# Layer one's input projection in another column order, with the compression products, turns and the compressed branch placed between its groups

## The reference

```python
proj = hn @ nsa_w_in                      # 2212 columns: q 768, kc vc ks vs kw vw 192 each, gates 36, memory q 256
q, ks, kw = rope(q), rope(ks), rope(kw)
kc = rope(compress(kc_raw)); vc = compress(vc_raw)     # 15 blocks of 32 tokens: gelu(x @ w1) @ w2
out = g0 * softmax(q kc) vc + g1 * softmax(q ks) vs + g2 * softmax(q kw) vw
mo  = softmax(q_mem mem_k) mem_v
h   = h + rmsnorm(concat(out, mo) @ w_out)
```

## Time and profile before

| what | value |
|---|---|
| median of 3 runs (lowest, highest) | 831.14 us (829.1, 834.99) |
| the profiled execution, its span | 830.26 us, 828.5 us |
| mean granted TensorE clock | 0.945 |
| busy: TensorE, VectorE, ScalarE, GpSimd | 754.0, 489.2, 407.2, 100.0 us |

### The profile page before, as it was taken

One profiled execution on the slowest core, in us unless ns is written; L12 is line 12 of the kernel. 1 busy time (PEld: TensorE's weight loads), 2 busy tenths in 40 slices (PEclk: granted clock), 3 DMA queues, 4 the chain that ended last, 5 costly groups with the idle time before them and its releaser, 6 DMA issues.

```text
span 828.5 us, 15559 instructions
## 1 busy us (share of the span) xinstructions
PE 754.0 (91%) x6725; PEld 653.9 (79%) x6725; DVE 489.2 (59%) x707; ACT 407.2 (49%) x644; POOL 100.0 (12%) x148
## 2 busy tenths in 40 slices
PE   4999856969999999999988976999989999999996
PEld 3888745657888888888868965999978888888885
DVE  5767653562686666643559696433456866666422
ACT  6744743553765554532767613332326845455411
POOL 4004042460000000000141003530000000000000
PEclk9999875789999999999989987899999999999999
DMA  9846600000765655555653323000006556555511
GB/s 301 297 131 207 222 29 1 1 1 9 233 210 184 203 173 183 203 191 164 186 183 102 107 98 103 3 4 5 4 2 229 169 187 203 171 185 203 183 71 52
DMA packets 78280, 111.74 MB, mean 135 GB/s; under 512 B 2125, under 2 KB 63715, under 8 KB 78211
## 3 DMA queue, kind: packets, MB, share of 16 engines
q1 hardware_dynamic: 77090, 107.67, 38.6%
q0 software_dynamic: 976, 3.04, 1.2%
q10 hardware_dynamic: 144, 0.04, 0.0%
HBM read 109.68 MB, written 1.05 MB: 134 GB/s over the span
## 4 chain that ended last, share of the span: by engine, by line
PE 68%; DVE 14%; ACT 6%; issue 2%; POOL 0%; DVEq 0%; ACTq 0%
PE ps L945 18%; PE ps L1084 10%; PE ps L947 9%; PE ps L666 8%; PE ps L667 7%; PE ps L668 7%; DVE w_lo L1688 3%; PE ps L821 2%; PE ps L795 1%; PE ps L772 1%; ACT scores L1327 1%; ACT w_hi L1251 1%; DVE row_max L1776 1%; DVE x_hi_lo L1913 1%; ACT x_hi_lo L1432 1%
## 5 line engine op out<-in xcount | busy, mean ns | idle before, releaser
L1688 DVE TENSOR_TENSOR w_lo<-w_raw,w_hi 128x2048 fp32r<-128x2048 f32 (+1 forms) x99 | 222.8, 2263 | 96.9 <-ACT w_hi L1251 96.7
L945 PE MATMUL ps<-x_hi_lo,w_hi 128*128 128x512 f32 x640 | 226.5, 399 | 0.0
L1251 ACT ACTIVATE w_hi<-w_raw 128x2048 fp32r<-128x2048 f32 (+1 forms) x99 | 185.4, 1890 | 50.7 <-PE ps L668 50.3
L947 PE MATMUL ps<-x_hi_lo,w_lo 128*128 128x256 f32 x640 | 179.7, 281 | 0.0
L945 PEld LDWEIGHTS ps<-x_hi_lo,w_hi 128*128 128x128 f32 x640 | 120.3, 188 | 29.9
L947 PEld LDWEIGHTS ps<-x_hi_lo,w_lo 128*128 128x128 f32 x640 | 120.9, 189 | 0.0
L666 PE MATMUL ps<-w_hi,x_hi_lo 128*128 128x512 f32 (+2 forms) x240 | 83.1, 346 | 3.5 <-DVE x_hi_lo L1913 3.0
L667 PE MATMUL ps<-w_lo,x_hi_lo 128*128 128x512 f32 (+2 forms) x240 | 81.6, 340 | 0.0
L668 PE MATMUL ps<-w_hi,x_hi_lo 128*128 128x512 f32 (+2 forms) x240 | 81.4, 339 | 0.0
L666 PE MATMUL ps<-w_hi,hidden_hi 128*128 128x512 f32 x176 | 68.6, 390 | 0.0
L667 PE MATMUL ps<-w_lo,hidden_hi 128*128 128x512 f32 x176 | 68.5, 389 | 0.0
(11 more groups left out here) (368 smaller groups left out, 1166.2 us busy)
## 6 DMA issues: line engine op xcount, KB each, us to landing
w_raw<-w_ffn_in SPq DMA_DIRECT2D x44, 1024.0 KB, 5.1
w_raw<-w_ffn_out SPq DMA_DIRECT2D x22, 1024.0 KB, 4.9
w_raw<-rwkv_w_in SPq DMA_DIRECT2D x11, 1024.0 KB, 5.4
w_raw<-nsa_w_in SPq DMA_DIRECT2D x8, 1024.0 KB, 12.1
w_raw<-w_out SPq DMA_DIRECT2D x8, 1024.0 KB, 5.0
w_raw<-w_mem_kv SPq DMA_DIRECT2D x2, 1024.0 KB, 8.4
w_raw<-nsa_cmp_k_w SPq DMA_DIRECT2D x2, 1024.0 KB, 5.4
w_raw<-nsa_cmp_v_w SPq DMA_DIRECT2D x2, 1024.0 KB, 5.4
```

Of the source, the lines that this page charges most:

```text
L945: pe.matmul(psum[:, bank + j, :], kt_of(w_hi, i, k)[:, c], xx[:, k, :, :].rearrange("p c n -> p (c n)"), start=k == 0, stop=False)
L947: ins = pe.matmul(psum[:, bank + j, 0:SEQ], kt_of(w_lo, i, k)[:, c], xh[:, k, :], start=False, stop=k == KD - 1)
L1251: act.activation(w_hi[:, i % SPL, 0:size(i)], raw[:, i % RAW, 0:size(i)], ACT.Copy).then_inc(hi_done, 1)
L1688: dve.tensor_tensor(w_lo[:, i % RAW, 0:size(i)], raw[:, i % RAW, 0:size(i)], w_hi[:, i % SPL, 0:size(i)], ALU.subtract).then_inc(lo_done, 1)
```

## The change

- The groups of the projection are `NSA_COLS` in the order 1, 2, 0, 4, 3: columns 512 to 1024, 1024 to 1536, 0 to 512, 1920 to 2212 (gates and memory queries, 292), and last 1536 to 1920 (window keys and values, 384). The compression's weights come before the last group, and so do its products, in banks 6 and 7.
- Turns stand at `between` points of the groups, by half and tile: memory keys in group 2, compression inputs in group 3, selected keys in group 4, queries between the two compression products, memory queries, `hidden_turns`, `block_mlp` and `block_key_turn` in group 5. A turn may have one column (`count`).
- The window keys are rotated after group 5 and turned in step 2 of the attention, through banks 4 and 5.
- The block scores move from step 4 to step 1, `block_probs` from 5 to 3, the block turns to steps 4 and 5, one tile each, both in bank 5.
- Memory outputs go to bank 6 + t.
- One weight piece and not three of the output projection is split before the attention; eight halves and not four are split within, from step 7 (VectorE) and not 12.
- The rotation order on VectorE, the copies of `vc_tok` on GpSimd, and the points of `turn_out` and `split_to` follow.

```diff
+NSA_COLS = [(0, 512), (512, 1024), (1024, O_KW), (O_KW, O_G), (O_G, NSA_IN)]
+NSA_ORDER = [1, 2, 0, 4, None, 3]
-        LAG_T, LAG_V, HALF_STEPS = 3, 4, 12
+        LAG_T, LAG_V, HALF_STEPS = 3, 4, 7
-                c = SEQ * (f - FT) + P * t
-                return 6, slice(c, c + P)
+                return 6 + t, slice(P * (f - FT), P * (f - FT) + P)
+        TURNS = [("mk", 0, 2), ("dup", 0, 2), ("dup", 2, 2), ("dup", 4, 2), ("dup", 6, 2), ("dup", 8, 1),
+                 ("q", 0, 2), ("q", 2, 2), ("q", 4, 2), ("mq", 0, 2), ("dup", 9, 2), ("dup", 11, 1)]
+        T_MK, T_CMP, T_KS, T_Q, T_MQ, T_KW = 0, (1, 2, 3), (4, 5), (6, 7, 8), 9, (10, 11)
+        GROUP_BANK = (4, 6, 4, 6, 4, 4)
...
@@ gpsimd
-            pool.wait_ge(tok_evA, 4)
+            pool.wait_ge(tok_evA, 3)
...
+            keys_twice(0)
             pool.wait_ge(kp_f, 2)
             pool.memset(sc[:], 0.0).then_inc(cmp_set, 1)
...
+            keys_twice(1)
@@ tensor
+                        if (hf, t) in between:
+                            between[hf, t]()
...
             def cmp_gemm(kv):
                 pe.wait_ge(kp_hi, kv + 1)
                 pe.wait_ge(kp_lo, kv + 1)
+                pe.wait_ge((tok_evA, tok_evD)[kv], 4)
...
                 for s in range(n + LAG_V):
+                    if layer == 0 and s == LAG_T:
+                        pe.wait_ge(tp0A, len(TURNS) // 2)
+                    if layer == 0 and s == NMEM:
+                        pe.wait_ge(tp0D, len(TURNS) // 2)
                     if s < n:
                         scores(layer, s)
                     if layer == 0 and s == 1:
-                        hidden_turns()
+                        block_scores()
                     if layer == 0 and s == 2:
-                        block_mlp()
+                        pe.wait_ge(dup_k, 8)
+                        pe.wait_ge(tok_evA, 6)
+                        pe.wait_ge(tok_evD, 6)
+                        for k in T_KW:
+                            turn(k)
...
+                    if layer == 0 and s in (NMEM, NMEM + 1):
+                        block_turns(s - NMEM)
...
+            token_gemm(2, xh, xl, {(0, 1): memory_keys})
+            token_gemm(3, xh, xl, {(0, 1): turns_of(dup_c, 4, T_CMP)})
+            token_gemm(4, xh, xl, {(0, 1): turns_of(dup_k, 4, T_KS)})
             cmp_gemm(0)
+            turns_of(roped_q, 1, T_Q)()
             cmp_gemm(1)
+            token_gemm(5, xh, xl, {(0, 0): memory_queries, (0, 1): hidden_turns, (1, 0): block_mlp, (1, 1): block_key_turn})
@@ scalar, attention
+                    if layer == 0 and s == 2:
+                        block_exps()
                     if s < n:
                         exps(layer, s)
+                    if layer == 0 and s == 2:
+                        turn_out(T_KW[0])
...
-                    if layer == 0 and s + 1 - HALF_STEPS in range(4):
-                        split_half(first["out", 0] + 3 + (s + 1 - HALF_STEPS) // 2, (s + 1 - HALF_STEPS) % 2)
+                    if layer == 0 and s + 1 - HALF_STEPS in range(8):
+                        split_half(first["out", 0] + 1 + (s + 1 - HALF_STEPS) // 2, (s + 1 - HALF_STEPS) % 2)
@@ vector, before the attention
+            turn_out(T_Q[1])
+            split_to(first["cmp"] + 6)
+            turn_out(T_MQ)
+            block_kv_out()
+            split_to(first["cmp"] + 7)
+            token_out(5)
...
+            rope_heads(O_KW, GROUPS, small, roped_k)
             attention(0)
```

More of the change, by code:

```diff
@@ L99, in weight_pieces @@
         out.append(kt_view(w_mem_kv)[:, 4 * hf:4 * hf + 4, :])
-    start["nsa"] = len(out)
-    for c in range(0, NSA_IN, 512):
-        for hf in range(2):
-            out.append(kt_view(nsa_w_in)[:, 4 * hf:4 * hf + 4, c:min(c + 512, NSA_IN)])
-    start["cmp"] = len(out)
-    for w in (w1k, w1v):
-        for hf in range(2):
-            out.append(kt_view(w)[:, 8 * hf:8 * hf + 8, :])
+    for c in NSA_ORDER:
+        if c is None:
+            start["cmp"] = len(out)
+            for w in (w1k, w1v):
+                for hf in range(2):
+                    out.append(kt_view(w)[:, 8 * hf:8 * hf + 8, :])
+        else:
+            start["nsa", c] = len(out)
+            for hf in range(2):
+                out.append(kt_view(nsa_w_in)[:, 4 * hf:4 * hf + 4, slice(*NSA_COLS[c])])
     for layer in range(2):
@@ L604, in scale_probs @@
                     ins.then_inc(a_p, 1)
-                    if layer == 0 and i == 1:
-                        pool.wait_ge(a_p, u + 1)
-                        pool.wait_ge(c_kd, 1)
-                        for j in range(1, 3):
-                            link(pool.tensor_copy(vcs[CPAD * j:CPAD * j + NCMP], vcs[0:NCMP]))
-                        pool.tensor_copy(vcs[CPAD * 3:CPAD * 3 + NCMP], vcs[0:NCMP]).then_inc(cmp_set, 1)
-                        pool.wait_ge(cmp_set, 2)
             scale_probs(0)
@@ L729, in token_gemm @@
                             ins.then_inc(tok_mm, 1)
-                            if g == 0:
+                            if p == 0:
                                 norm(1)
-                    ins.then_inc(used, 1)
+                        if t == TT - 1:
+                            ins.then_inc(used, 1)
+                        if (hf, t) in between:
+                            between[hf, t]()
             def turn(k):
-                if k >= 4:
+                if 4 <= k < T_KW[0]:
                     pe.wait_ge((tp0A, tp0D)[k % 2], (k - 4) // 2 + 1)
-                for j in range(2):
-                    kind, n = TURNS[2 * k + j]
+                kind, n0, count = TURNS[k]
+                for j in range(count):
+                    n = n0 + j
                     for t in range(TT):
@@ L2016, in _ @@
             dve.wait_ge(trig_s, 1)
-            for g in range(1, 6):
-                i = first["nsa"] + 2 * (g - 1)
+            for p in range(1, 5):
+                i = group(p)[0]
                 split_to(i + 3 + AHEAD)
-                if g == 4:
-                    turn_out(1)
+                if p == 3:
+                    turn_out(T_CMP[0])
+                    turn_out(T_CMP[2])
                     block_inputs(0)
                     block_inputs_lo(0)
-                if g == 5:
+                if p == 4:
@@ L2045, in _ @@
-            turn_out(9)
+                    rope_heads(0, HEADS, [rtq[:, k] for k in range(4)], roped_q)
+            dve.wait_ge(tok_evA, 5)
+            dve.wait_ge(tok_evD, 5)
+            dve.tensor_tensor(gates[:], pr[:, :, O_G:O_G + GATES], gateb[:].unsqueeze(1).to_broadcast([P, TT, GATES]),
+                              ALU.add).then_inc(gl_s, 1)
+            turn_out(T_Q[1])
[3 more added lines that the diff above has]
+            split_to(first["cmp"] + 7)
```

240 lines of the change are left out of this document (115 added, 125 removed).

## The result

| | before | after |
|---|---|---|
| median (lowest, highest) | 832.35 us (829.1, 834.99), 4 runs | 806.76 us (805.28, 808.76), 4 runs |
| profiled execution, its span | 830.26 us, 828.5 us | 808.76 us, 807.0 us |
| mean granted TensorE clock | 0.945 | 0.963 |

The medians are 25.6 us apart. The ratio is 0.9704, with a 95% interval of 0.9674 to 0.9734, which makes 24.6 us of 832.35; 18.0 was forecast. The two profiled executions differ by 21.5.

What follows compares the result with a forecast made beforehand. It took TensorE's own work to bound the projection, and waits (largest on bank 6) and 1.2 GHz the attention. 7.7 won, 5.1 given back, 14.5 and 2.4 won, 1.5 set against: 18.0 us less, 812.3 (813 beside the median), range 804 to 824.

Steps and rivals of the forecast that it cites:

- projection to the first scores: Layer one's projection: regrouped columns and spread turns bring the first scores at 93.8 us, not 101.48; 7.7 us won.
- opening, to the first NSA scores: Start of layer one's attention: VectorE's work and the window keys' turns leave 2.6 of the 7.7 us lead.
- to the first output product: Layer one's attention from step 4: about 14.5 us won in steps 4 to 10, 2.4 after; output product at 164.7.
- set against margins: Projection: 1.5 us added because VectorE's last weight pieces are only 0.4 to 1 us ahead, and for semaphore time.
- From there on both kernels have the same pieces in the same order: Behind layer one's first output product: same pieces, split equally far ahead, so no further gain counted.
- all after it shifted by one constant: Sign in the profile after: everything behind the first output product, near 165 to 167 us, moves by the same amount.
- a clock of 1.00 without a break: Sign in the profile after: TensorE's granted clock stays at 1.00 from 28.8 to about 97 us.
- rival 2: Attention: the clock returns at once with dense steps 4 to 6; 3 to 4 us more won, 809; chance 0.10.
- rival 1: Attention: the clock stays at 1.2 GHz throughout; 8 us lost, 821; chance 0.17.
- 3 (a longer opening): Opening: handovers among four engines around the window keys take 6 us more, 819; chance 0.13.
- 5 (banks that don't free the values): Attention: VectorE's queue position still holds the values; the 14.5 us shrinks to some 7, 820; chance 0.05.
- 4, the slower one: Projection: VectorE and ScalarE can't keep the new order, pieces 8 to 15 come late; 26 us, 839; chance 0.05.

Runs made afterwards that it cites:

- b_again: The kernel before, unchanged, run once more for a second profile: 834.42 us in one run.
- a_again: The changed kernel, unchanged, run once more for a second profile: 804.72 us, ratio 0.9689.
- b_banks: The kernel before with only the memory outputs alternating between banks 6 and 7, both block turns sharing bank 5: 818.24 us, ratio 0.9827.
- a_bank6: The changed kernel with all memory units' outputs in bank 6 again: 817.94 us, ratio 0.9844.
- a_shift: The changed kernel with VectorE's eight half remainders one step later, ScalarE's halves where they were: 798.43 us, ratio 0.959.
- a_late16: The changed kernel with VectorE's last weight remainder moved from before the window keys to behind the copy of their turn: 803.25 us, ratio 0.9656.
- a_split12: The changed kernel with three output projection pieces split ahead of the attention and four halves from step 12, as before: 806.49 us, ratio 0.9686.
- a_warm: The changed kernel with the last weight remainder moved behind the window keys' turn copy, plus eight unused 512-column products in TensorE's gap: 804.21 us, ratio 0.9653.

## Why the prediction was right, and where it wasn't

It gave 813.0 us in a range of 804 to 824; 806.76 came. In parts, as time won in us, beside the two pairs of profiles (before and after, `b_again` and `a_again`):

| part | forecast | first pair | second pair |
|---|---|---|---|
| ahead of the first product of `nsa_w_in` | 0 | -1.93 | 0.25 |
| projection to the first scores | 7.7 | 6.98 | 7.56 |
| opening, to the first NSA scores | -5.1 | -6.03 | -5.34 |
| to the first output product | 16.9 | 18.65 | 20.60 |
| to the join | 0 | -1.30 | 1.98 |
| behind the join | 0 | 5.13 | 5.72 |
| set against margins | -1.5 | | |
| sum | 18.0 | 21.5 | 30.8 |

The sign and the waits it named in layer one were right: more product time saved than the opening gives back, and the steps of the attention freed of the waits on bank 6. Its picture of the clock was wrong, and it left out layer two. In turn:

**The step that failed** is the sentence behind the first output product, "From there on both kernels have the same pieces in the same order", and with it "all after it shifted by one constant". `out_cols` is called for both layers, and unit 0 to 3 of layer two are memory units too. So the edit that I costed in steps 4 to 10 of layer one acts a second time, and what lies behind the join gets shorter: by 5.1 us in the first pair of profiles, 5.7 in the second. `b_banks` shows it without the rest of the change (603.7, 5.1 less than the kernel before), `a_bank6` shows it gone (607.9, 4.2 more than the changed kernel). It is the largest part of what the forecast was short by; the rest is the steps up to the output product, 1.8 and 3.7 us, and the 1.5 of margins. Between the output product and the join nothing holds from pair to pair.

**Projection.** 65.0 us was forecast from the first product to the first scores (28.8 to 93.8). It is 65.7 in all eleven profiles of the new projection, and 72.7 to 73.3 in the three of the old one: 7.0 to 7.6 won. What spreads the first scores inside each group (94.3 to 97.8, and 101.5 to 104.4) lies ahead of the stage. The clock comes up to stay between 14.2 and 22.6 us, and the first product of `nsa_w_in` starts between 28.6 and 32.1, by and large the later the clock comes up; until then the memory's products of 512 columns are 0.43 us apart (`a_shift`, 17.1 to 21.8), from then on 0.23. (The profile has no record of the clock ahead of its first rise; there the products' spacing tells it.) In the first pair that costs the changed kernel 1.93 us, which is why its first scores are 5.05 us sooner and not 7. Of the rest the interpolated widths held (0.134 predicted for 292 columns; rows in the changed kernel are 0.13 and 0.14 apart) and so did "a clock of 1.00 without a break". The 1.5 us for VectorE's margins wasn't needed: the one wait, of 0.46 us, is the 0.6 between the first two groups that the sum already has.

**Opening.** 5.1 us given back was the forecast. From the first scores to the first NSA scores it is 7.2 and 7.9 us before, 13.2 in both profiles after: 5.3 to 6.0. It was sized right, and its cause as written: the window keys' chain over four engines, and VectorE's queue. One weight remainder taken out of it makes it 1.6 us shorter (`a_late16`), two put in make it 4.4 longer (`a_split12`). 2.6 us of lead were to be left; -1.0 and 2.5 are.

**Steps 4 to the output product.** 58.7 us was forecast (106.0 to 164.7) for 75.6; 56.9 and 55.0 came. The banks are 7.2 of the 18.7 (`a_bank6`); alone in the kernel before they are worth 11.2 (`b_banks`). The chain of the half splits was read rightly in kind: I wrote steps of 5.0 and 3.4, then 6.0 and 3.9, and they are 5.0 and 3.1, then 6.0 to 7.0 and 3.6 to 3.9. VectorE's step 7 was forecast for 120.8 and began at 120.02, step 10 for 134.2 and began at 133.11, and step 15's maxima, forecast for about 158, are at 157.26. That these hit is partly luck: the first NSA scores came at 109.63 and not 106.0 (1.9 us of it from ahead of the projection, 0.7 in it, 1.0 in the opening), and the maxima of steps 4 to 7 were 2.1 to 2.7 us apart, where I had steps of 3.8 to 4.6 at 1.2 GHz. The split of the gain into 14.5 up to step 10 and 2.4 behind it can't be worked out from the prediction's own step times; the total of 16.9 can. What I took for a given of the kernel was a fault of the change: with VectorE a step later it is gone (`a_shift`, 8.3 us). Moving two pieces' splits from before the attention into it was worth nothing with that fault in it (`a_split12`); without it nobody ran the comparison.

**The clock.** I took 1.2 GHz from 97.5 to about 131. It is there from 102.1 to 112.3, then in two pieces of 3.4 us (129.4 to 132.8, 146.4 to 149.9) and from 156.7 to 170.3; in `a_again` from 101.8 to 115.4, 129.1 to 135.9 and 149.6 to 153.0. So rival 2 (809) was the nearer description of the clock, and rival 1 fell, which the Trainium skill's rule on transposes (TensorE: Matmul & The Clock Gate, section PE-mode transpose) spoke for: with the same quarter of turns the second tile's steps ran at 0.80 in the changed kernel (133.1 to 166.5), and in `a_shift` only 3.4 us of them were at 1.2 GHz. That the rule was no danger to the projection the trace had said before, and 1.00 over 28.8 to 94 agrees. From step 7 on VectorE's and ScalarE's chains set the steps, so that the clock gave little there; `a_warm` shows the same for the opening.

**The other rivals.** 3 (a longer opening) meant 18 us from the first scores to the first NSA scores, where 12.2 was forecast and 13.2 came; 5 (banks that don't free the values) would have left waits behind L1846 in layer one, and none is left. 4, the slower one, would have shown as new waits between 28.8 and 94, and there is none. Of the signs that the prediction named, the first scores missed 93 to 96 by 0.4 us (96.43; the late start of the projection), the first NSA scores missed 106, and the output product (166.57) lies in 165 to 167.

**Open.** Of the 2.9 us that layer two's attention gets shorter, 1.4 are waits for the remainder that are gone. Why the clock behind layer two's attention depends on the banks is only argued: with less idle time in the attention it comes back before the chunk products begin. No run held the attention's length and changed the idle time alone. Nor did a run put the block scores and probabilities back into steps 4 and 5: that they are the 11.4 us of layer one's 18.7 that `a_bank6` leaves is argued, from the 5.60 us wait and the 4.11 us of the 48 products in the kernel before. How much of the opening is VectorE's block probabilities wasn't measured either, only that a faster clock shortens it (11.6 us in `a_late16`) by no more than 0.5 us by VectorE's maxima and 1.0 by the scores.

## What to carry to other kernels

Look for every caller of a helper that the diff touches, in every layer, before writing that the rest is the same: here a placement made for one stage was worth a fifth of the gain in another. When one engine's instruction in a step needs another engine's last one of the same step, count that as a chain through the step, and try it a step later: that was worth 8.3 us here, a third of what the whole change brought. Measure a stage from its own first instruction: from the start of the span the projection's gain is 5.05 us in one pair and 7.81 in the other, from its first product 6.98 and 7.56. And take a second profile of each kernel: it tells a difference that comes and goes (ahead of the projection) from one that stays (behind the join).

## What the runs showed of the hardware

In the kernel before, the clock fell within the 48 products of 15 columns (112.2 to 116.3, the fall at 113.6) although TensorE counted as busy throughout. TensorE had also been idle for 0.88 and 1.23 us shortly before them (up to 108.6 and 111.1), and no run changed one without the other, so which of the two it was stays open. In the changed kernel the same products are at 97.4 to 100.2, and the clock falls at 102.1, behind an idle 1.62 us; it stays down 10.2 us there and 13.7 in `a_again`, not 41.

In the kernel before it stayed at 1.2 GHz from 113.6 to 154.5 with TensorE busy 29.45 of these 40.90 us; in the changed kernel it was at 0.92 on average over 113 to 154 with 32.43 of 41.00 busy. In `b_banks`, with 8.1 us less of the waits behind the remainder, the stretches at 1.2 GHz between the first NSA scores and the output product add up to 25.8 us and not 46.8.

The same instructions in the same order had their slow stretches in other places from one execution to the next: ahead of the projection, where TensorE's instructions are the same in all fourteen profiles, the clock came up to stay anywhere from 14.2 to 22.6 us.
